# Row mix and norm of the first block joined in one stage

## The reference, cut to what matters

```python
m = (g[:, :, 0] * (y_rnn @ w_br_rnn[l])
     + g[:, :, 1] * (y_diff @ w_br_diff[l])
     + g[:, :, 2] * (y_fox @ w_br_fox[l]))
x = x + m @ w_out[l]                    # the "row mix": 1024x1024 times 1024x1024
h = rmsnorm(x, norm2_g[l])              # the norm: per row, x * rsqrt(mean(x*x) + eps) * gain
u = causal_dwconv(h @ ffn_up[l], ffn_conv_w[l], ffn_conv_b[l])
```

## Time and profile before

| | us |
|---|---|
| median of 3 executions | 3448.46 |
| lowest, highest | 3443.95, 3450.4 |
| the profiled execution, its own time | 3449.72 |
| its span in the trace | 3448.0 |
| PE busy in it | 3143.5 (91%) |
| stage_rows, matmuls and adds | 1362 to 1452 |
| stage_norm_to_channels | 1453 to 1484 |

### The profile page before, as it was taken

How to read it: one execution, slowest core, us unless ns; L and a number is a source line. 1 busy time by engine, 2 the same in 40 slices (tenths; PEclk the granted TensorE clock), 3 DMA queues, 4 the chain that set the end, 5 groups by cost and what they waited for, 6 DMA issues and landing times. The chain is left out here.

```text
span 3448.0 us, 40113 instructions
## 1 busy us (share of the span) xinstructions
PE 3143.5 (91%) x15115; PEld 2562.8 (74%) x15115; DVE 1419.9 (41%) x2250; ACT 1123.2 (33%) x1466; POOL 753.2 (22%) x482
## 2 busy tenths in 40 slices
PE   8999899899899799879999999968799888899988
PEld 6777777687777587768888888756777777778866
DVE  4355133311135312234344434472443445465666
ACT  4344143312156422132223122151332344324332
POOL 2000100022211121121122122411522232212342
PEclk9999999999999899989999999977899999899989
DMA  3100210022121123141111111034032110212223
GB/s 125 52 25 1 68 31 22 11 65 65 58 53 44 32 73 116 43 72 43 36 61 43 43 43 61 0 116 61 17 110 94 31 31 25 98 38 66 82 80 116
DMA packets 275400, 194.00 MB, mean 56 GB/s; under 512 B 66504, under 2 KB 246856, under 8 KB 275280
## 3 DMA queue, kind: packets, MB, share of 16 engines
q1 hardware_dynamic: 273168, 191.33, 19.5%
q10 hardware_dynamic: 2112, 1.05, 0.1%
HBM read 165.77 MB, written 26.57 MB: 56 GB/s over the span
## 5 line engine op out<-in xcount | busy, mean ns | idle before, releaser
L136 POOL TENSOR_TENSOR w_low<-w_raw,w_high 128x1024 fp32r<-128x1024 f32 (+1 forms) x178 | 410.5, 2306 | 1939.5 <-ACT w_high L129 1935.0
L154 PE MATMUL pu<-act_high,w_high 128*128 128x512 f32 x704 | 276.8, 393 | 12.9 <-POOL w_low L136 9.3
L154 PE MATMUL pu<-act_low,w_high 128*128 128x512 f32 x704 | 275.9, 392 | 0.0
L154 PE MATMUL pu<-act_high,w_low 128*128 128x512 f32 x704 | 275.9, 392 | 0.0
L129 ACT ACTIVATE w_high<-w_raw 128x1024 fp32r<-128x1024 f32 (+1 forms) x178 | 177.1, 996 | 277.1 <-PE py L154 92.8
L154 PE MATMUL pg<-act_high,w_high 128*128 128x512 f32 x512 | 202.1, 395 | 28.8 <-ACTq L615 24.5
L154 PE MATMUL pg<-act_low,w_high 128*128 128x512 f32 x512 | 200.9, 392 | 0.0
L154 PE MATMUL pg<-act_high,w_low 128*128 128x512 f32 x512 | 200.4, 392 | 0.0
L639 DVE TENSOR_TENSOR gate<-gate,py 128x1024 f32<-128x1024 f32 x24 | 29.3, 1222 | 389.9 <-PE py L154 389.9
L154 PEld LDWEIGHTS pu<-act_high,w_high 128*128 128x128 f32 x704 | 133.6, 190 | 41.8 <-POOL w_low L136 9.9
L1631 DVE TENSOR_TENSOR x<-x,pd 128x512 f32<-128x512 f32 x176 | 117.9, 685 | 93.6 <-PE pd L1560 93.6
(11 more groups left out here) (636 smaller groups left out, 7521.8 us busy)
## 6 DMA issues: line engine op xcount, KB each, us to landing
w_raw<-in_w_in SPq DMA_DIRECT2D x106, 512.0 KB, 4.1
w_raw<-in_ffn_up SPq DMA_DIRECT2D x44, 512.0 KB, 3.8
w_raw<-in_w_out SPq DMA_DIRECT2D x24, 512.0 KB, 4.5
v_raw<-in_ffn_down SPq DMA_DIRECT2D x11, 1024.0 KB, 5.0
decay<-acum_rows SPq DMA_DIRECT2D x16, 512.0 KB, 3.7
x_ring<-in_x SPq DMA_DIRECT2D x8, 512.0 KB, 9.4
m_part<-gate SPq DMA_DIRECT2D x8, 512.0 KB, 3.0
w_raw<-in_w_br_rnn SPq DMA_DIRECT2D x8, 512.0 KB, 6.4
```

Source lines behind the costliest of these rows:

```text
L136: pool.tensor_tensor(self.low[slot][:, 0:nk, :], self.raw[slot][:, 0:nk, :], self.high[slot][:, 0:nk, :].bitcast(F32), ALU.subtract).then_ ...
L154: last = pe.matmul(out[:, h, :] if not halves else out[h], w[slot][:, k, :], x[:, k, cols], start=(n == 0), stop=(n == 3 * nk - 1))
```

## The change

`stage_rows` and `stage_norm_to_channels` are replaced by one stage, `stage_rows_norm`. Half 0 of the product is computed as before, tile by tile over all row blocks. The four tiles of half 1 are all split into resident tiles of their own, `RH` and `RL`, while half 0 runs. Half 1 is then computed row block by row block, `rest(b)`: 24 matmuls into bank b % 4 over the four resident tiles. As soon as a row block is complete, DVE adds it (line 724 of the changed kernel), ACT squares it and takes the root (653, 655), DVE takes the reciprocal and scales (728, 732), and PE turns it (696) one row block later, behind `rest(b + 1)`, into banks 4 to 7. The gain, squares and scaled rows lie where `m` was, which is free once it is split. `x` is loaded in 8 DMAs of 0.5 MB, and the first two tiles of `w_out` to be loaded go ahead of it. There is one barrier less. The number of matmuls, transposes and elementwise instructions is the same.

```diff
-def stage_norm_to_channels(core, src_tile, gain_vec, src_dram=None, ahead=()):
...
-def stage_rows(core, XH, XL, nk, w, acc, whole=None, load_acc=None, add=True):
...
+def stage_rows_norm(core, w, X, x_dram, gain_vec, ahead):
...
+            def _(sp):
+                for t in range(2, NG):
+                    W.load(sp, t % 2, t // 2, src[t])
+                for b in range(NB):
+                    sp.dma_start(X[:, b, :], x_dram[steps(b), :]).then_inc(sem(f"x_loaded{b}"), 16)
+                for t in range(NG, 2 * NG):
+                    W.load(sp, t % 2, t // 2, src[t])
+                sp.wait_ge(sem("m_low"), KD)
+                sp.dma_start(gain[:, :], gain_vec.partition_broadcast(P)).then_inc(sem("gain_loaded"), 16)
+                for slot in range(2):
+                    sp.wait_ge(W.s("raw_free", slot), NG + 1)
+                A.load(sp)
...
+            def _(pool):
...
+                for r in range(NG):
+                    t = NG + r
+                    pool.wait_ge(sem("rest_high"), r + 1)
+                    pool.tensor_tensor(RL[r][:, :, :], W.raw[t % 2][:, :, :], RH[r][:, :, :].bitcast(F32), ALU.subtract).then_inc(sem("rest_low"), 1)
+                    pool.wait_ge(sem("rest_low"), r + 1)
+                    pool.sem_inc(W.s("raw_free", t % 2), 1)
+                A.split_low(pool)
...
+            def _(act):
...
+                for r in range(NG):
+                    t = NG + r
+                    act.wait_ge(W.s("loaded", t % 2), 16 * (t // 2))
+                    act.activation(RH[r][:, :, :], W.raw[t % 2][:, :, :], ACT.Copy).then_inc(sem("rest_high"), 1)
+                act.wait_ge(sem("out"), NB)
+                A.split_high(act)
...
+                for b in range(NB):
+                    if b >= 2:
+                        high(b - 2)
+                    act.wait_ge(sem("whole"), b + 1)
+                    act.activation(squares[:, :], X[:, b, :], ACT.Square, accum_out=stats[:, 0, b:b + 1]).then_inc(sem("squared"), 1)
+                    act.wait_ge(sem("squared"), b + 1)
+                    act.activation(stats[:, 1, b:b + 1], stats[:, 0, b:b + 1], ACT.Sqrt, scale=1.0 / D, bias=core.eps[:, 0:1]).then_inc(sem("root"), 1)
+                high(NB - 2)
+                high(NB - 1)
...
+                def rest(b):
+                    pe.wait_ge(sem("added"), b + 1)
+                    if b >= 4:
+                        pe.wait_ge(sem("whole"), b - 3)
+                    for kk in range(KD):
+                        r, k = kk // G, kk % G
+                        if b == 0 and k == 0:
+                            pe.wait_ge(sem("rest_low"), r + 1)
+                        for i, (x, v) in enumerate(((AH, RH), (AL, RH), (AH, RL))):
+                            last = pe.matmul(banks[:, b % 4, :], x[:, kk, steps(b)], v[r][:, k, :],
+                                             start=(kk == 0 and i == 0), stop=(kk == KD - 1 and i == 2))
+                    last.then_inc(sem("rest"), 1)
...
+                def turn(b):
+                    pe.wait_ge(sem("scaled"), b + 1)
+                    pe.wait_ge(sem("added"), NB)
+                    if b >= 2:
+                        pe.wait_ge(sem("low"), b - 1)
...
+                for b in range(NB):
+                    rest(b)
+                    if b:
+                        turn(b - 1)
+                turn(NB - 1)
...
+                for b in range(NB):
+                    cols = two_halves[1]
+                    dve.wait_ge(sem("rest"), b + 1)
+                    dve.tensor_tensor(X[:, b, cols], X[:, b, cols], banks[:, b % 4, :], ALU.add).then_inc(sem("whole"), 1)
+                    if b >= 2:
+                        low(b - 2)
+                    dve.wait_ge(sem("root"), b + 1)
...
+                low(NB - 2)
+                low(NB - 1)
...
-        stage_rows(core, core.AH, core.AL, KD, w_out, X, whole=core.M, load_acc=io["x"][0])
-        stage_norm_to_channels(core, X, io["norm2_g"][0], ahead=columns(io["ffn_up"][0], 0, D_FF))
+        stage_rows_norm(core, w_out, X, io["x"][0], io["norm2_g"][0], columns(io["ffn_up"][0], 0, D_FF))
```

More of the change, by code:

```diff
@@ L695, in _ @@
                 W.open_pe(pe)
-                for t, (half, kg) in enumerate(tiles):
+                for t in range(NG):
                     W.wait(pe, t % 2, t // 2)
                     for b in range(NB):
-                        if half and kg == 0:
-                            pe.wait_ge(sem("added"), b + 1)
-                        steps = slice(b * P, (b + 1) * P)
                         for k in range(G):
[L703 to L709, removed]
-                            last.then_inc(sem("out"), 1)
-                    last.then_inc(W.s("used", t % 2), 1)
+                            kk = t * G + k
+                            if b == 0:
+                                pe.wait_ge(sem("m_low"), kk + 1)
+                            for i, (x, v) in enumerate(((AH, W.high), (AL, W.high), (AH, W.low))):
+                                last = pe.matmul(banks[:, b, :], x[:, kk, steps(b)], v[t % 2][:, k, :],
+                                                 start=(kk == 0 and i == 0), stop=(kk == KD - 1 and i == 2))
+                        if t == NG - 1:
+                            last.then_inc(sem("out"), 1)
+                    if t < NG - 1:
+                        last.then_inc(W.s("used", t % 2), 1)
@@ new lines, in turn @@
+                def turn(b):
[3 more added lines that the diff above has]
+                        pe.wait_ge(sem("low"), b - 1)
+                    for k in range(KD):
+                        last = pe.transpose(turned[b % 2][:, k, :], scaled[b % 2][:, k * P:(k + 1) * P], ident[:, :])
+                    last.then_inc(sem("turned"), 1)
+                for b in range(NB):
+                    rest(b)
+                    if b:
+                        turn(b - 1)
@@ L713, in _ @@
+                turn(NB - 1)
             @block.vector
             def _(dve):
[L715 to L728, removed]
-                        if add:
-                            dve.tensor_tensor(acc[:, b, cols], acc[:, b, cols], out[:, b, :], ALU.add).then_inc(sem("added"), 1)
-                        else:
-                            dve.tensor_copy(acc[:, b, cols], out[:, b, :]).then_inc(sem("added"), 1)
+                for k in range(KD):
+                    dve.wait_ge(sem("m_high"), k + 1)
+                    dve.tensor_tensor(AL[:, k, :], M[:, k, :], AH[:, k, :].bitcast(F32), ALU.subtract).then_inc(sem("m_low"), 1)
@@ new lines, in _, with low @@
+                for b in range(NB):
+                    cols = two_halves[0]
+                    dve.wait_ge(sem(f"x_loaded{b}"), 16)
+                    dve.wait_ge(sem("out"), b + 1)
+                    dve.tensor_tensor(X[:, b, cols], X[:, b, cols], banks[:, b, :], ALU.add).then_inc(sem("added"), 1)
+                dve.wait_ge(sem("gain_loaded"), 16)
+                def low(b):
+                    dve.wait_ge(sem("high"), b + 1)
+                    dve.tensor_tensor(AL[:, :, steps(b)], turned[b % 2], AH[:, :, steps(b)].bitcast(F32), ALU.subtract).then_inc(sem("low"), 1)
@@ new lines, in _ @@
+                for b in range(NB):
+                    cols = two_halves[1]
[4 more added lines that the diff above has]
+                    dve.wait_ge(sem("root"), b + 1)
+                    dve.reciprocal(stats[:, 2, b:b + 1], stats[:, 1, b:b + 1]).then_inc(sem("rstd"), 1)
+                    dve.wait_ge(sem("rstd"), b + 1)
+                    if b >= 2:
+                        dve.wait_ge(sem("turned"), b - 1)
+                    dve.scalar_tensor_tensor(out=scaled[b % 2][:, :], in0=X[:, b, :], scalar=stats[:, 2, b:b + 1], in1=gain[:, :],
+                                             op0=ALU.mult, op1=ALU.mult).then_inc(sem("scaled"), 1)
```

36 lines of the change are left out of this document (24 added, 12 removed).

## The result

The changed kernel takes 3428.4 us (median of 5 runs, 3425.4 to 3432.87), the kernel before 3448.46: 20.1 us less, a ratio of 0.9946 with an interval of 0.9931 to 0.996. 3429 was forecast. Its profiled execution has a span of 3428.3 us against 3448.0.

The account below looks back on a forecast made before the run. PE was taken to bound the kernel. New stage end 1407.95 + 43.5 + 5.3 + 0.5 + 7.3 = 1464.6 against 1484.3, gain 19.7, called 20, off 3449.7 less 1.3 for the median: 3429 us, range 3422 to 3438.

Parts of the forecast that it names:

- What bounds: Whole kernel: PE carries the program; between row mix and norm, 32.8 us hold no matmul of the product.
- PE's stream, what stays: Half 1: the same 192 matmuls in 43.5 us, 5.44 us per row block, reordering costed at 0.
- PE's stream, what is added: Half 1: six groups of 8 transposes between matmuls, 0.88 us each, 5.3 us; upper bound 1.98 each, 11.9 us.
- rival 1: Half 1: transpose groups cost 1.98 us, or each turn about a microsecond; gain 12 to 13, 3436 us; chance 0.15.
- The wait of a transpose: Half 1: add-to-scaling chain of 3.8 us under 6.3 us of PE work, 2.5 us left, so transposes don't wait.
- The first row block: Start of half 1: chain 5.1 us with table load, cover 5.44; scaling meeting POOL's split adds 0.5 us (0 to 2.0).
- The resident tiles: During half 0: the four split tiles ready at about 1392.2 to 1405, before half 1 starts at 1407.9; no matmul waits.
- The tail: Behind the last row block's matmuls: 7.3 us to the last low part, or 8.1 with transposes at the lower clock.
- the prediction's paragraph on transposes: Last transposes: the full clock does not engage for transposes, giving 8.1 us behind the last matmuls and gain 19.1, not 19.9.
- Behind the seam: Feed-forward stage: its load list hangs on the barrier alone, so it moves as a whole and takes no gain back.
- Rival 3: Feed-forward or later stage: something not starting at the barrier takes the 20 us back, 3445 to 3450 us; chance 0.04.
- Rival 2: Half 1: PE pauses each round, clock falls to 0.50, row block 12.2 us, not 6.3; 3476 us; chance 0.03.

Follow-up runs that it names:

- run with the order alone: Changed kernel with half 1 row block by row block over resident tiles, but the norm again a separate stage behind a barrier; 3445.6 us, 0.9997 of before.
- run without cover: Changed kernel with each turn(b) directly behind its own rest(b), not behind the next row block's matmuls; 3470.38 us, 1.0068 of before.
- run of the loads on both kernels: Feed-forward stage's loads reordered, third and fourth weight tiles first: 3426.91 us on the changed kernel, 3446.0 on the one before.
- run with transposes in the middle: Changed kernel with PE waiting for the scaled rows directly behind rest(b), transposes 12 matmuls later inside rest(b + 1); 3471.31 us, 1.0067 of before.

## Why the prediction was right

- *What bounds.* The seam was 32.8 us without a matmul of the product. The run with the order alone keeps 32.5 of them (1450.77 to 1483.29) and gains nothing.
- *PE's stream, what stays.* 5.44 us per row block were forecast at no cost for the new order. Between the first two adds, with no transposes, it is 1417.00 - 1411.63 = 5.37, and the run with the order alone has 43.45 us for the eight.
- *PE's stream, what is added.* 0.88 us per group from a row of another stage; 0.87 measured at one group, and 6.34 - 5.44 = 0.90 from add to add. The bound from the stage's own rows, 1.98, was one of the lower clock, and so rival 1 (3436 us) did not come.
- *The wait of a transpose.* The chain was to be 3.8 us and 2.5 of its cover left: the run without cover shows a wait of 3.81, and two more scalings (2.6) nearly fit.
- *The first row block.* 0.5 us were taken for a collision with POOL; there was none. The `ffn_up` tiles were to land together after 6.6 us. They landed after 3.9 and 6.5, so POOL began with the first one earlier, and its second low part ended at 1413.3, before the scaling at 1415.40. That scaling ended at 1416.68, with 0.1 us to spare before `turn(0)` at 1416.80. So the end at 0 of the stated 0 to 2.0 is what came; that the transposes of the first block did not wait was close.
- *The resident tiles.* The last low part was to end at 1405, ended at 1402.7, and with the 1.8 us of shift this is 1404.5.
- *The tail.* 7.3 us from PE's end to the last low part forecast, 1462.27 - 1455.08 = 7.2 measured. `turn(7)` ran at the higher clock (1.09 us) after 2.93 us of waiting, so 7.3 and not the 8.1 to which the prediction's paragraph on transposes would have led. (By the prediction's own sum, the gains set against each other there are 18.9 and 19.7, not 19.1 and 19.9.)
- *Behind the seam.* From the next stage's first DMA to the end it was 1963.1 us before and is 1964.8 now; the repeated run of the changed kernel has 3426.7 - 1465.27 = 1961.4, so 1.7 us is within what two traces of one kernel differ by. Rival 3 did not come, and the run of the loads on both kernels shows nothing of it either.
- *Slower.* Rival 2 needed pauses, and there were none. With pauses of 3.8 us the kernel takes 3470, 22 us more than before. That this lies near the rival's 3476 is chance: the rival had 47 us from a clock of 0.50 throughout, and the run has, against the changed kernel, 10 from the clock and some 31 from standing still. The expectations of both runs with pauses were wrong in having the clock stay up.

The sum was 19.7 us for the stage, and it is 20.2: 0.5 from the collision that did not come and 0.1 from the tail, less 0.1 for the six groups, which took 5.4 us in place of 5.3. The gap at the barrier, which the sum did not have, grew by 0.6 us, outside the stage.

## What to carry to other kernels

A stage that only turns and normalises what a matmul stage has just made can lie beside that stage, if the matmuls are ordered so that outputs become complete one after the other and not all at the end; the order itself costs nothing where the operand that all of them share fits resident. Count the chain behind one output and set it against the matmuls of the next: 3.8 against 6.3 us here, and a design with the same parts but no output in between was slower than the two separate stages. Leave some of the cover unused: where PE had to wait 2.2 us in a round, its clock fell in two of three cases. A price for such an interleaving is to be read where the engine already runs at the clock that it will have.

## What the runs showed of the hardware

- Waits of PE and its clock. In half 1, the clock fell to 0.50 around the first wait of each run that has one of 4.94 to 5.31 us. In the run without cover it fell around five of the six later waits of 3.81, in the run with transposes in the middle around all six of 3.85 to 3.90. In the run with four more scalings it fell around a wait of 2.21 and one of 2.24 and stayed at 1.00 around another of 2.21; it also stayed around one of 2.30 in the run with two more. So in these runs the length of the wait alone does not tell which way it goes. `turn(7)` of the changed kernel still ran at the higher clock after 2.93 us, but over 1459 to 1460 the clock was 0.91, and 0.50 from 1460 on.
- Small loads can hold SP's queue as long as large ones. The last `lam<-in_s_log_step`, 4 KB, took SP 7.6 us to issue; its kind landed after a median of 17.9 us, the tiles of 512 KB after one of 9.1, and the pair asked for behind it after 14.2 and 15.2. Moving the tiles ahead was worth 7.5 us of the whole kernel (3426.91 to 3419.46, on two chips, with 3449.27 and 3448.8 for the kernel before).
